# Router logits in four column groups and a reordered routing chain in a two-layer hybrid attention and expert kernel

## What is computed

```python
def expert_choice_ffn(h, p):
    cap = CAPACITY_FACTOR * n // N_EXPERTS          # 32 of the sample, 16 of the prompt
    aff = softmax(xs @ p['w_router'])               # n x 16
    gate, idx = lax.top_k(aff.T, cap)
    xe = xs[idx]
    hg = einsum('ecd,edf->ecf', xe, p['w_gate'])
    hu = einsum('ecd,edf->ecf', xe, p['w_up'])
    ye = einsum('ecf,efd->ecd', silu(hg) * hu, p['w_down']) * gate[..., None]
    return zeros_like(xs).at[idx].add(ye)

def trunk_layer(x, cond, p, ...):
    mod = silu(cond) @ p['w_ada'] + p['b_ada']      # shift1, scale1, gate1, shift2, scale2, gate2
    h = rmsnorm(x, p['norm1']) * (1 + scale1) + shift1
    x = x + gate1 * attention_branches(h, ...)      # ends in merged @ w_out
    h = rmsnorm(x, p['norm2']) * (1 + scale2) + shift2
    return x + gate2 * expert_choice_ffn(h, p)
```

## Time and profile before

| | us |
|---|---|
| median of 3 runs | 1909.35 |
| lowest, highest | 1907.31, 1909.38 |
| the profiled execution, its time | 1909.12 |
| the profiled execution, its span | 1907.3 |

### The profile page before, as it was taken

The page is one execution under the profiler, slowest core; times in us unless marked ns, Lnnn a source line. Parts: engine busy times, 40 slices in busy tenths (PEclk is TensorE's granted clock), DMA queues, the critical chain, the costliest instruction groups (busy, mean ns, idle before and its releaser), DMA issues.

```text
span 1907.3 us, 21463 instructions
## 1 busy us (share of the span) xinstructions
PE 1760.6 (92%) x8548; PEld 972.3 (51%) x8548; DVE 671.7 (35%) x1375; ACT 325.6 (17%) x811; POOL 320.7 (17%) x349
## 2 busy tenths in 40 slices
PE   6999999999999988889889999999999999898886
PEld 3656777894533323233255587778844333332322
DVE  1135556752412212122132455567424131221212
ACT  2232223320301001010032322222112010100101
POOL 0216455330000000000002437533200000000000
PEclk9999999999899999999999999999999999999999
DMA  9235132139499999999961642313448999999997
GB/s 389 84 143 235 70 130 78 67 136 412 184 428 427 431 428 429 430 429 429 427 246 71 236 159 94 122 46 131 196 202 331 429 430 428 430 429 429 428 429 294
DMA packets 58289, 541.14 MB, mean 284 GB/s; under 512 B 7048, under 2 KB 7496, under 8 KB 14416
## 3 DMA queue, kind: packets, MB, share of 16 engines
q1 hardware_dynamic: 56656, 535.65, 67.7%
q0 software_dynamic: 1536, 4.13, 0.6%
HBM read 536.54 MB, written 3.21 MB: 283 GB/s over the span
## 4 chain that ended last, share of the span: by engine, by line
PE 78%; DMA 12%; DVE 4%; SPq 3%; ACT 2%; issue 1%; DVEq 0%; ACTq 0%
PE banks L2300 25%; PE banks L1863 10%; PE banks L1825 8%; DMA arena<-in_w_exp 7%; PE banks L1915 7%; PE banks L2219 4%; PE banks L1717 4%; PE banks L1887 4%; SPq L678 3%; PE banks L2379 3%; DMA ring<-in_w_exp 3%; PE banks L2088 1%; PE banks L2275 1%; DMA ring<-in_w_att 1%; PE banks L1772 1%; PE banks L2029 1%
## 5 line engine op out<-in xcount | busy, mean ns | idle before, releaser
L2300 PE MATMUL banks<-arena 128*64 128x512 f32 x1680 | 378.9, 595 | 31.5 <-DMA arena<-in_w_exp 19.7
L2300 PE MATMUL banks<-ring,arena 128*64 128x512 f32 x1392 | 314.9, 598 | 21.0 <-DMA ring<-in_w_exp 10.9
L2300 PEld LDWEIGHTS banks<-arena 128*64 128x64 f32 x1680 | 116.6, 137 | 272.2 <-issue 217.5
L2300 PEld LDWEIGHTS banks<-ring,arena 128*64 128x64 f32 x1392 | 97.7, 138 | 220.9 <-issue 179.4
L1654 DVE TENSOR_TENSOR arena<-banks,arena 32x512 f32<-32x512 f32 (+1 forms) x128 | 87.9, 687 | 266.0 <-PE banks L2300 264.6
L1825 PE MATMUL banks<-ring,arena 128*128 128x384 f32 (+1 forms) x512 | 161.7, 476 | 1.8 <-ACT arena L930 1.8
L1717 PE MATMUL banks<-arena 128*128 128x128 f32 (+3 forms) x740 | 106.2, 278 | 31.5 <-DVE arena L1639 18.6
L1717 PEld LDWEIGHTS banks<-arena 128*128 128x128 f32 (+3 forms) x740 | 83.0, 140 | 94.0 <-issue 41.3
L1825 PEld LDWEIGHTS banks<-ring,arena 128*128 128x128 f32 x512 | 97.2, 192 | 61.7 <-issue 2.7
L1915 PE MATMUL banks<-arena,ring 128*128 128x384 f32 x384 | 126.8, 488 | 0.0
L1138 ACT ACTIVATE arena<-banks 128x512 f32<-128x512 f32 x32 | 19.1, 597 | 511.7 <-PE banks L2300 511.7
(11 more groups left out here) (251 smaller groups left out, 2051.5 us busy)
## 6 DMA issues: line engine op xcount, KB each, us to landing
arena<-in_w_exp SPq DMA_DIRECT2D x69, 2048.0 KB, 30.6
ring<-in_w_exp SPq DMA_DIRECT2D x69, 2048.0 KB, 29.5
ring<-in_w_att SPq DMA_DIRECT2D x80, 1024.0 KB, 6.7
arena<-in_w_exp SPq DMA_DIRECT2D x72, 1024.0 KB, 27.2
ring<-in_w_exp SPq DMA_DIRECT2D x36, 1024.0 KB, 14.1
ring<-in_w_att SPq DMA_DIRECT2D x26, 768.0 KB, 8.2
arena<-in_w_att SPq DMA_DIRECT2D x12, 1024.0 KB, 11.5
ring<-in_w_att SPq DMA_DIRECT2D x8, 672.0 KB, 15.2
```

Source lines behind the costliest of these rows:

```text
L2300: ins = pe.matmul(PS[64 * h:64 * h + 64, bank], lhs(k), slots[i][:, c0:c0 + BF], start=k == 0, stop=k == KC - 1)
```

## The change

Six things are changed.

1. The logits are computed in two steps. `router_parts` has 8 matmuls with 32 columns of `WA` stationary and the tokens (`H2[:, k]`, 128 columns) moving. k = 0 to 3 go to the four groups of 32 columns of TensorE, and so to four groups of 32 rows of bank 5, and k = 4 to 7 are added onto these. ScalarE copies the result (`PARTS`, 128x128). `router` is one matmul that adds the four groups with a constant of ones, `FOLD`. The first four matmuls wait for ScalarE's half of `H2` only.
2. `h2_turn` signals its first four transposes apart (`h2_half`), and ScalarE's copy waits for these alone. For the prompt the copy stands ahead of ScalarE's square. Every copy of the parts stands behind the root, and ahead of the `WARM` exponential.
3. TensorE's order in `out` for the prompt: the first `router` behind k = 0, the second behind the first matmul of k = 3, `affinity_turn` behind the first of k = 4.
4. Pieces of modulation: `next_ada(4, 5)` (layer 0) and `gain(0, 2)` (layer 1) stand ahead of `position_turn(l, 0)`. Piece 5 of `ada` goes between `router_parts` and `router` of the prompt; pieces 6 and 7 stay behind the sample gathers.
5. The scaled prompt rows `XN2[:, 0]` are written by ScalarE, behind the prompt's exponential, and no longer by VectorE. As they read `RS` later, the softmax's reciprocal goes into `ST`.
6. The two zeroings stand behind the prompt's dispatch.

```diff
@@ h2_turn, router @@
-                    ins = settle(turn(PS[:, 2 * min(n, 1) + c // 4, P * (c % 4):P * (c % 4) + P],
-                                      X[:, LATE[n], P * c:P * c + P]))
+                    ins = turn(PS[:, 2 * min(n, 1) + c // 4, P * (c % 4):P * (c % 4) + P], X[:, LATE[n], P * c:P * c + P])
+                    if c == 3:
+                        ins.then_inc(h2_half.s, 1)
+                    elif c < KC - 1:
+                        settle(ins)
                 ins.then_inc(h2_mm.s, 1)

-            def router(l, n):
-
+            def router_parts(l, n):
+                if n:
+                    pe.wait_ge(parts_ok.s, parts_ok.at(l, n))
+                elif l + 1 < DEPTH:
+                    pe.wait_ge(gain_row.s, gain_row.at(l, 1))
                 pe.wait_ge(h2_act.s, h2_act.at(l, n + 1))
-                pe.wait_ge(h2_dve.s, h2_dve.at(l, n + 1))
-                t = LATE[n]
-                bank, col = 0, NE * max(t - 1, 0)
+                s = min(LATE[n], 1)
                 for k in range(KC):
-                    ins = pe.matmul(PS[:, bank, col:col + NE], H2[:, k], WA[:, min(t, 1), k],
-                                    start=k == 0, stop=k == KC - 1)
+                    if k == 4:
+                        pe.wait_ge(h2_dve.s, h2_dve.at(l, n + 1))
+                    j = 32 * (k % 4)
+                    q = k - (k % 4 == 3)
+                    ins = pe.matmul(PS[j:j + 32, 5, 0:P], WA[:, s, q:q + 2], H2[:, k], start=k < 4, stop=k >= 4)
...
+                ins.then_inc(parts_mm.s, 1)
+
+            def router(l, n):
+
+                pe.wait_ge(parts_ok.s, parts_ok.at(l, n + 1))
+                col = NE * max(LATE[n] - 1, 0)
+                ins = settle(pe.matmul(PS[:, 0, col:col + NE], PARTS, FOLD, start=True, stop=True))
@@ TensorE, out for the prompt and after @@
-                router(l, 0)
+                router_parts(l, 0)
...
+                        if (k, h) == (3, 0):
+                            router(l, 1)
+                        if (k, h) == (4, 0):
+                            affinity_turn(l, 0)
...
+                    if k == 0:
+                        router(l, 0)
                     if k == 1:
                         h2_turn(l, 1)
                     if k == 2:
-                        router(l, 1)
-                    if k == 3:
-                        affinity_turn(l, 0)
+                        router_parts(l, 1)
...
+                if l + 1 == DEPTH:
+                    gain(0, 2)
+                else:
+                    next_ada(4, 5)
                 position_turn(l, 0)
                 if l + 1 == DEPTH:
-                    gain(0, 5)
+                    gain(2, 5)
                 h2_turn(l, 2)
-                if l + 1 < DEPTH:
-                    next_ada(4, 5)
-                else:
+                if l + 1 == DEPTH:
                     gain(5, KC)
+                router_parts(l, 2)
+                next_ada(5, 6)
                 router(l, 2)
...
-                next_ada(5, KC)
+                next_ada(6, 7)
                 if l + 1 == DEPTH:
                     pe.wait_ge(gain_row.s, gain_row.at(l, 1))
                     gather_sample(0, 5)
+                next_ada(7, KC)
                 position_turn(l, 1)
@@ ScalarE @@
                 for n, t in enumerate(LATE):
+                    if n == 2:
+                        h2_out(l, n)
                     act.wait_ge(x1_ok.s, x1_ok.at(l, n + 1))
...
-                    h2_out(l, n)
+                    if n < 2:
+                        h2_out(l, n)
                     act.wait_ge(ms_t.s, ms_t.at(l, n + 1))
                     nc.scalar.activation(RS[:, t:t + 1], RS[:, t:t + 1], ACT.Sqrt).then_inc(root_t.s, 1)
+                    act.wait_ge(parts_mm.s, parts_mm.at(l, n + 1))
+                    nc.scalar.copy(PARTS, PS[:, 5, 0:P]).then_inc(parts_ok.s, 1)
...
+                    if n == 2:
+                        nc.scalar.activation(XN2[:, 0], X[:, 0], ACT.Identity, scale=RS[:, 0:1]).then_inc(xn_t.s, 1)
@@ VectorE @@
-                    nc.vector.tensor_scalar(XN2[:, t], X[:, t], r, None, ALU.mult).then_inc(xn_t.s, 1)
+                    if i < 2:
+                        nc.vector.tensor_scalar(XN2[:, t], X[:, t], r, None, ALU.mult).then_inc(xn_t.s, 1)
...
-                    link(nc.vector.reciprocal(rs, st), l)
+                    link(nc.vector.reciprocal(st, st), l)
...
                 affinities(1)
-                nc.vector.memset(YS[1], 0.0)
-                nc.vector.memset(XG[:, KC * GE * CAP:], 0.0).then_inc(pad_ok.s, 1)
                 positions(1)
                 positions_out(1)
                 dispatch_part(0, 0, 1).then_inc(disp_ok.s, 1)
+                nc.vector.memset(YS[1], 0.0)
+                nc.vector.memset(XG[:, KC * GE * CAP:], 0.0).then_inc(pad_ok.s, 1)
```

More of the change, by code:

```diff
@@ L61 @@
 C_LAM = C_IOTA + CAP_S
-C_W = C_LAM + 2 * DEPTH
+C_FOLD = C_LAM + 2 * DEPTH
+C_W = C_FOLD + NE
 def lam_init(layer):
@@ L94, in constants @@
         c[:, C_LAM + 2 * layer + 1] = 1.0 - lam_init(layer)
+    for j in range(4):
+        c[32 * j + NE * (j == 3):32 * j + NE * (j == 3) + NE, C_FOLD:C_FOLD + NE] = np.eye(NE)
     return c
@@ L476, in backbone @@
         H2 = at(0, KC, P)
+        PARTS = at(9504, P)
         FNG = at(11744, D)
@@ L521, in backbone @@
         IDT = CST[:, C_ID:C_ID + P]
+        FOLD = CST[:, C_FOLD:C_FOLD + NE]
         ONES = CST[:, C_ONE:C_ONE + P]
@@ L582, in backbone @@
         h2_mm, h2_act, h2_dve = sem("h2_mm", NT), sem("h2_act", NT), sem("h2_dve", NT)
+        h2_half, parts_mm, parts_ok = sem("h2_half", NT), sem("parts_mm", NT), sem("parts_ok", NT)
         ht_mm, ht_act, ht_dve = sem("ht_mm", NT), sem("ht_act", 4 * NT), sem("ht_dve", 4 * NT)
@@ L934, in h2_out @@
             def h2_out(l, n):
-                act.wait_ge(h2_mm.s, h2_mm.at(l, n + 1))
+                act.wait_ge(h2_half.s, h2_half.at(l, n + 1))
                 nc.scalar.copy(H2[:, 0:4].rearrange("p c n -> p (c n)"), PS[:, 2 * min(n, 1)]).then_inc(h2_act.s, 1)
@@ L1553, in affinities @@
                     link(nc.vector.reduce_sum(st, lg, AX), l)
-                    link(nc.vector.reciprocal(rs, st), l)
+                    link(nc.vector.reciprocal(st, st), l)
                     nc.vector.tensor_tensor(AFF[:, t0:t0 + nt], lg,
-                                            rs.rearrange("p (t o) -> p t o", o=1).to_broadcast([P, nt, NE]),
+                                            st.rearrange("p (t o) -> p t o", o=1).to_broadcast([P, nt, NE]),
                                             ALU.mult).then_inc(aff_ok.s, 1)
```

## The result

The changed kernel takes 1898.27 us (median of 4 runs, 1896.23 to 1900.48) against 1908.67 of the kernel before, run beside it: ratio 0.9945, 95% interval 0.9930 to 0.9961. A second set of runs gave 1896.63 against 1908.82, 0.9936 (0.9925 to 0.9948). The forecast was 1898.2. The total agrees; two of its steps don't.

The account below looks back on a forecast made before the run. Layer 0 was taken to end with the weight stream, restarted after modulation piece 4, and layer 1 a fixed time after its first expert matmul. 1909.12 - 8.1 - 2.8 = 1898.2 us, range 1894.5 to 1903.5.

Parts of the forecast that it names:

- The restart carries layer 0: Layer 0 ends with the weight stream, which restarts once modulation piece 4 is used, 8.1 us earlier: term -8.1.
- The bar: Layer 0: the first expert must start by 521.7, 3.9 us earlier than before, to keep the whole 8.1 us.
- the routing chain is second there: Layer 0: the first expert matmul, 14.6 us behind the stream's restart, comes second to the stream in ending the layer.
- Sizes in the way to the restart: Layer 0, TensorE from `out` for tile 2 to piece 4's end: 17.98 us, with parts 0.85 and router 0.21 each.
- The rule against it: Tiling-mode changes drain TensorE: by the rule a dozen edges at 0.1 us lose 1.2 us; by the row, free.
- Layer 0's first expert: Layer 0: first expert near 517, 8.6 us earlier; at half clock near 523, past the latest allowed start.
- early fall: Rival: layer 0's clock falls early and stays low, the first expert is late, the stream stalls; 1901.4, chance 0.14.
- Layer 1: Layer 1 ends a fixed time after its first expert; its routing chain gets 2.75 earlier at the prompt gathers: term -2.8.
- the table load in the way: Layer 1: the warming exponential's table load (1.28) now stands behind the copy of the parts and costs 0.6 us.
- clock kept: Rival: the clock stays up in layer 1's prompt gathers, layer 1 gives -4.9; 1896.1, chance 0.18.
- Slower: Rival: small groups pull the clock down over the prompt's `out`, 13.7 us in each layer; 1925.6, chance 0.05.

Follow-up runs that it names:

- e1: The changed kernel with piece 4 of the next layer's modulation (layer 0) back behind the prompt's transposes: 1903.85 us, ratio to the kernel before 0.9973.
- e4: The changed kernel with the two zeroings back ahead of the prompt's positions, run twice: the second time 1900.70 us, ratio to the kernel before 0.9957.
- e2: The kernel before, with only piece 4 (layer 0) and gain pieces 0 and 1 (layer 1) moved ahead of the position turn: 1904.59 us, 0.9985.
- e3: The changed kernel with the logits in the old groups of 8 matmuls, no parts, copy or fold, all moves kept: 1905.94 us, 0.9989.
- e5: The changed kernel with layer 0's modulation piece 4 ahead of the output projection, so its slot holds no load: 1899.20 us, 0.9952.
- e7: The changed kernel with 14 idle matmuls ahead of layer 0's first expert: 1902.79 us, ratio to the kernel before 0.9969.
- e9: The changed kernel with 6 idle matmuls in layer 1 and the wait for `out`'s second bank ahead of that bank's own first matmul: 1895.32 us, 0.9931.
- after_again: The changed kernel, unaltered, profiled and timed again: 1896.63 us, ratio to the kernel before 0.9936.

## Why the prediction was right, and where it was not

- **The restart carries layer 0: right, as one of two clocks.** The term was -8.1, measured -7.3: the restart came 7.7 earlier and so did the last group, but from the last group to the next anchor it took 0.43 longer (454.98 before, 455.41 after). No edit lies there, and the thirteen profiles have between 455.0 and 456.4. e1 shows the restart alone: the restart 5.0 later, the layer 4.65 longer.
- **The bar was wrong.** I held that nine units could be loaded from the restart on and that the tenth only needs the first expert unit used, so a first expert up to 19.3 us behind the restart would cost nothing. The stream stays whole at 14.4 and 14.7 (after, before), is 0.6 late at 15.0 (2.0 in the first execution of e4), 1.2 at 15.9, 2.1 at 16.4, 3.7 at 17.9 and 4.8 at 19.4. What I had not read are the loads behind the tenth unit. SyncE has a row of three loads around the first expert (first row below, of the changed kernel). The second is the tenth unit's, and it does go out when the first unit is used, at 523.1. The third brings two units at once, into the slots of expert units 2 and 3, and can't go out before unit 3 is used, with the first 32 expert records (7.02 us): the row ends 7.7 us behind the first expert, here, before and in e1, e2, e3, e5 and e7.

```profile
519.50 9.39 SPq L684 DMA_DIRECT2D arena<-in_w_exp  x3
...
540.45 2.00 SPq L684 DMA_DIRECT2D arena<-in_w_exp  x2
```

  The tightest is the second load behind that row, the first of the two in the second row. By the order in `placed` it brings units 23 and 24, into the slots of expert units 4 and 8, and unit 8 is used only by the third matmul block: the load goes out 19.25 us behind the first expert (19.27 before, 19.26 in e7). The fourteen units between the restart and it are 34.3 us of stream, at the prediction's 2.45 each. So the first expert may stand some 15.0 us behind the restart; this is an estimate, and the losses above begin there. In e7 this load goes out 2.9 us too late by that count, and the last group came 3.7 later.

  The corner was in the trace before: there, the first expert was 14.6 behind the restart and I took that for slack. So "the routing chain is second there" was false; both had to move by 8, and both did. With the old groups and the early restart (e3) only 1.2 of the 7.3 was left, in an execution that was at half clock ahead of the first expert. That the total came out all the same is luck in this step: the prediction asked only 3.9 of the chain, and it gained 8.0. With 3.9 layer 0 would have ended about 4 us later by the two clocks (37.3 + 437.5 = 474.8, against 470.6).
- **Sizes in the way to the restart.** 18.0 us forecast for the end of piece 4, 18.4 measured: parts 0.64 instead of 0.85 and a fold 0.13 instead of 0.21 (two of each, -0.6), but `out` cost more. It waits 0.26 for VectorE (the residual of the tile before), which the old group of 1.69 had covered: the shorter cover was not costed. And four records of `out` take 1.96 behind the parts and 1.81 behind the fold, where four clean ones take 1.72.
- **The rule against it.** I took the edges for free from the gain pieces' row. The rows above show 0.24 behind the first parts (0.19 in e9, where no wait stands between) and 0.19 behind the second (1.05 for two records, 0.86 clean): 0.4 us a layer. The 0.09 behind each fold is no part of it: it stood behind the old group too (8 records of `out` in 3.53, 3.44 clean; first row below). And my row was not clean: the 8 transposes behind the 40 records of gain pieces took 1.02, 0.15 over the clean 0.87 (second row).

```profile
486.09 3.53 PE banks L2219 x8
...
1439.83 1.02 PE banks L1717 x8
```

  The Trainium skill, "TensorEngine Tiling (Array Packing)", section "Key Properties", says that a change of tiling mode drains TensorE, without a price; I had put 0.1 us for each of a dozen edges, 1.2 in all, with no row for the 0.1; measured, the edges behind the parts cost 0.8 in both layers. That a drain is the cause is argued from the place of the excess, no run isolates it.
- **Layer 0's first expert** 8.0 earlier against 8.6. The third group at half clock, as before, would have spoiled it, and that was a rival (early fall, 1901.4): after_again shows that it happens in some executions of this very kernel, with 1.8 us in that one.
- **Layer 1** -4.2 at the first expert (-4.9 at the last group) against -2.8. Up to the prompt gathers 2.81 against 2.75, so the chain was right with its errors cancelling: the copy 0.27 instead of 0.35, the clearing worth 0.63 (e4) instead of 0.75, the table load in the way as told. The rest is the clock, which fell only behind the gathers' first 12 records (1.55 us, before 2.82): the rival "clock kept" came half true. Of the -4.9, 0.8 lies behind the first expert (434.19 us to the last group before, 433.41 after). No edit lies there, and the thirteen profiles have between 432.4 and 434.6, so this part is scatter as far as is known.
- **Slower** (half clock over the prompt's `out`) did not come: 1.00 there in every stretch read.
- **The median.** 8.1 + 2.8 = 10.9 forecast; -12.2 behind the start in the profiled pair; medians 10.4 and 12.2 apart. The close hit of 1898.2 has a share of luck in it: layer 0 is over by 0.8, layer 1 short by 1.4 to 2.1.

## What to carry to other kernels

When a stream of weights restarts at one event and is next held by another, write both times with what follows each, and compute which is later. Go down the list of the loads behind the restart, each with the event that frees its slot: the next one need not be the tightest. The one that seems slack may be exactly level. When a group gets shorter, look at what it had covered: here a bank that VectorE frees. And where TensorE pauses ahead of a chain of small matmuls, try work that is due anyway in the pause, or idle matmuls: with them the granted clock stayed at 1.00 in both executions here, which the medians are too coarse to show.

## What was not expected of the hardware

- A group of 8 fp32 matmuls with 32 stationary and 128 moving columns takes 0.57 to 0.64 us between matmuls of `out`, 0.04 a record; behind other 32-column pieces the chain gives its 16 records 0.44 (e1) to 0.48. That is a third of the old 1.69, or a little over.
- The granted clock falls at different places in executions of one program: in layer 1 the first expert of kernels with the same instructions there moved between 33.1 and 35.1 us behind the anchor (34.25, 33.59, e7's 34.13, e1's 35.09 and, with all at full clock, e5's 33.12), in layer 0 between 33.16 and 35.15.
- The anchor of layer 0 moved by 5.8 us between executions (482.24 to 488.04), more than most single edits here are worth. Short intervals inside one execution (anchor to restart, anchor to first expert at an equal clock) told edits of 0.3 us apart; over a whole expert stage they scatter by 1 to 2 us; the ratios of medians here have 1.7 to 3 us of uncertainty either way.
